# Experts of a two-layer trunk: rows 4 to 7 of down loaded directly behind rows 0 to 3

## The reference

```python
def _expert_choice_ffn(h, router, w_gate, w_up, w_down):
    b, t, _ = h.shape
    cap = CAPACITY_FACTOR * t // N_EXPERTS
    aff = jax.nn.softmax(jnp.einsum('btd,de->bte', h, router).astype(jnp.float32), axis=-1)
    top_w, top_i = lax.top_k(jnp.swapaxes(aff, 1, 2), cap)
    bidx = jnp.arange(b)[:, None, None]
    xe = h[bidx, top_i]
    a = jnp.einsum('becd,edf->becf', xe, w_gate)
    u = jnp.einsum('becd,edf->becf', xe, w_up)
    y = jnp.einsum('becf,efd->becd', jax.nn.silu(a) * u, w_down) * top_w[..., None].astype(h.dtype)
    return jnp.zeros_like(h).at[bidx, top_i].add(y)
```

## Time and profile before

| | us |
|---|---|
| median of 3 runs | 3843.08 |
| lowest, highest | 3839.8, 3844.74 |
| the profiled execution's run | 3849.27 |
| its span, first to last instruction | 3847.5 |

### The profile page before, as it was taken

One profiled execution on the slowest core, in us unless ns is written; L12 is line 12 of the kernel. 1 busy time (PEld: TensorE's weight loads), 2 busy tenths in 40 slices (PEclk: granted clock), 3 DMA queues, 4 the chain that ended last, 5 costly groups with the idle time before them and its releaser, 6 DMA issues.

```text
span 3847.5 us, 59293 instructions
## 1 busy us (share of the span) xinstructions
PE 3193.2 (83%) x24115; PEld 2288.9 (59%) x24115; DVE 2297.4 (60%) x2989; ACT 1735.3 (45%) x2289; POOL 397.6 (10%) x100
## 2 busy tenths in 40 slices
PE   6899977866949999999978999777668588888887
PEld 1365767755426666666633666677553466666665
DVE  0141465577247887888831233656772688888887
ACT  1111431222127777777720114312222477777776
POOL 0000000000011222221100000000000133332222
PEclk9999978856969999999999999778558789889889
DMA  7310000000158999999964110000013589999996
GB/s 247 108 60 33 1 1 3 3 2 2 44 210 321 352 355 354 358 352 354 357 247 142 45 55 1 1 3 3 2 45 121 217 337 346 341 349 349 351 344 255
DMA packets 180704, 680.24 MB, mean 177 GB/s; under 512 B 15435, under 2 KB 25759, under 8 KB 180383
## 3 DMA queue, kind: packets, MB, share of 16 engines
q1 hardware_dynamic: 166088, 637.81, 43.5%
q0 software_dynamic: 6144, 20.98, 2.4%
q10 hardware_dynamic: 8283, 18.67, 1.2%
HBM read 656.44 MB, written 20.97 MB: 176 GB/s over the span
## 4 chain that ended last, share of the span: by engine, by line
PE 57%; DVE 16%; ACT 9%; issue 9%; DMA 7%; ACTq 1%; SPq 0%; DVEq 0%; POOL 0%; PEldq 0%
PE ps L718 13%; PE ps L1865 10%; PE ps L1835 7%; PE ps L1290 5%; ACT hi L1947 4%; PE ps L1635 4%; DMA gu<-in_moe_w_up 3%; PE ps L657 3%; PE ps L973 2%; DMA arena<-in_w_mod 2%; ACT arena L1956 2%; DVE gu_lo L2098 2%; DMA gu<-in_moe_w_gate 2%; PE ps L1873 1%; PE ps L951 1%
## 5 line engine op out<-in xcount | busy, mean ns | idle before, releaser
L2098 DVE TENSOR_TENSOR gu_lo<-gu,hi 128x2816 fp32r<-128x2816 f32 x256 | 783.5, 3091 | 273.4 <-ACT hi L1947 249.6
L1947 ACT ACTIVATE hi<-gu 128x2816 fp32r<-128x2816 f32 x256 | 643.7, 2550 | 141.6 <-DMA gu<-in_moe_w_up 115.3
L1835 PE MATMUL ps<-hi,xsplit 128*96 128x512 f32 (+3 forms) x2304 | 562.9, 390 | 45.4 <-DVE arena L2112 20.5
L718 PE MATMUL ps<-arena 128*128 128x512 f32 (+2 forms) x1536 | 503.4, 488 | 7.1 <-PE ps L718 4.3
L1835 PEld LDWEIGHTS ps<-hi,xsplit 128*96 128x96 f32 (+1 forms) x2304 | 396.0, 177 | 159.9 <-ACT hi L1947 28.4
L2098 DVE TENSOR_TENSOR down_lo<-down,hi 128x1024 fp32r<-128x1024 f32 (+1 forms) x256 | 403.9, 1620 | 45.7 <-ACT hi L1947 45.7
L1835 PE MATMUL ps<-gu_lo,xsplit 128*96 128x512 f32 (+3 forms) x1536 | 381.3, 384 | 54.5 <-DVE gu_lo L2098 54.3
L718 PEld LDWEIGHTS ps<-arena 128*128 128x128 f32 x1536 | 289.7, 190 | 212.3 <-issue 187.0
L1947 ACT ACTIVATE hi<-down 128x1024 fp32r<-128x1024 f32 (+1 forms) x256 | 344.0, 1377 | 158.2 <-PE ps L1865 158.2
L1835 PEld LDWEIGHTS ps<-gu_lo,xsplit 128*96 128x96 f32 (+1 forms) x1536 | 262.1, 177 | 150.7 <-DVE gu_lo L2098 92.6
L2180 POOL DMA_INDIRECT arena<-xn_rows,row_of x32 | 88.0, 2751 | 2158.0 <-DVE row_of L2089 2153.3
(11 more groups left out here) (290 smaller groups left out, 4443.9 us busy)
## 6 DMA issues: line engine op xcount, KB each, us to landing
gu<-in_moe_w_gate SPq DMA_DIRECT2D x256, 704.0 KB, 14.9
gu<-in_moe_w_up SPq DMA_DIRECT2D x256, 704.0 KB, 5.0
down<-in_moe_w_down SPq DMA_DIRECT2D x64, 2048.0 KB, 13.5
arena<-in_w_mod SPq DMA_DIRECT2D x24, 2048.0 KB, 8.0
down<-in_moe_w_down SPq DMA_DIRECT2D x32, 1536.0 KB, 17.0
arena<-in_w_in SPq DMA_DIRECT2D x6, 2048.0 KB, 8.0
arena<-in_w_out SPq DMA_DIRECT2D x4, 2048.0 KB, 10.2
arena<-in_w_in SPq DMA_DIRECT2D x4, 1536.0 KB, 6.6
```

The source lines that it names most:

```text
L718: ins = nc.tensor.matmul(out, lhsT=lhs, rhs=rhs, start=(f == 0), stop=(f == KT - 1))
L1835: ins = nc.tensor.matmul(ps[0:lhs.shape[1], 3 * m + b, 0:n], lhsT=lhs, rhs=w[:, c0 + 512 * b:c0 + 512 * b + n], start=(row == 0 and stage ...
L1947: nc.scalar.activation(hi_part(p, is_last), whole(p), ACT.Copy).then_inc(hi_a.sem, 1)
L2098: nc.vector.tensor_tensor(lo_part(p), whole(p), hi_part(p, is_last).bitcast(F32), ALU.subtract) \
```

## The change

In the loop and behind it, SP's call `downs(e, 1)` moves up: from behind `gate_up(e + 1, 1)` in the loop, and from behind `gate_up(NE - 1, 7)` at the end, to directly behind `downs(e, 0)`.

```diff
             with sp.Fori(1, NE - 1) as e:
                 downs(e, 0)
+                downs(e, 1)
                 gate_up(e, 6)
                 gate_up(e, 7)
                 gate_up(e + 1, 0)
                 gate_up(e + 1, 1)
-                downs(e, 1)
                 downs(e, 2)
                 for k in range(2, 6):
                     gate_up(e + 1, k)
             downs(NE - 1, 0)
+            downs(NE - 1, 1)
             gate_up(NE - 1, 6)
             gate_up(NE - 1, 7)
-            downs(NE - 1, 1)
             downs(NE - 1, 2)
```

## The result

The changed kernel takes 3854.76 us (median of 8 runs, 3839.36 to 3862.54); the kernel before, run beside it, 3843.68 (median of 8). The ratio is 1.0028, with a 95% interval of 1.0015 to 1.0041. So it is 11 us slower, and clearly so. 3843 was forecast, no change, with a range up to 3855: the time lies at the range's very end, 0.24 us inside it, and it moved where no move was forecast.

The account below looks back on a forecast made before the run. Prediction: the expert stages lean on both PE and DMA, neither full, with ACT alone waiting for weights. All terms summed to 0 on the 3847.5 us span; from the three-run median of 3843.08 it gave 3843 us, range 3834 to 3855.

Parts of the forecast that it names:

- What bounds the kernel, and where the queue stands still: Both expert stages: PE and DMA both lean, neither full; the DMA engines stand nearly still once per expert.
- Removed from the old place: 0.: Behind k1': d1 leaving moves later transfers up 5.1 us, but nobody waits for them; gain 0.
- The wait at the new place: 0.: SP's queue behind d0: d1's wait ends 8.0 and 7.4 us before k6's release, delaying nobody; 0.
- The transfer, first layer: 0.: Ahead of k6: d0 comes 5.1 us earlier, d1 takes 5.1, the 2.7 us hole stays; change 0.
- The transfer, second layer: -6 to +9, taken as 0.: Ahead of k6: room 5.3 us against 5.1 needed; -6 to +9 us over 15 experts, taken as 0.
- the bound for a lagging transfer: Second layer's k6: some 0.6 us later if one of sixteen DMA engines lags as in the first layer.
- k6 queues behind d1: Second layer: d0 no earlier, k6 1.4 us late for each of 15 experts; 21 us, 3864 us; chance 0.07.
- about as much as it is late: PE behind ACT's wait for k6: a delay of k6 costs PE about as much as it is late.
- the likeliest case: Whole kernel: nothing moves that anyone waits for; 3843 us, bounds 3837 to 3852; chance 0.82.
- a lower rate of d1: Second layer: d1 served at 350 GB/s takes 6.0 us, 0.7 over the room; 10 us, 3853 us; chance 0.03.
- The gate pairs land earlier.: First layer: k0' and k1' land earlier without d1; at most 20.6 us of gate waits go, 3822 us; chance 0.07.

Follow-up runs that it names:

- the half: Against the kernel before: d1 cut in two in both layers, only the second layer's first half moved ahead of k6; 3844.67 us, ratio 1.0006.
- the kernel with both fillers: Against the kernel before: 6 unused matmuls ahead of the gate's transposes and 12 ahead of the first down group, second layer; 3799.44 us, 0.9878.
- e2: Against the kernel before: d1 moved in the second layer's stage alone; 3851.68 us, ratio 1.0024.
- e9: Against the kernel before: d1 cut in two in both layers, three quarters moved ahead of k6 in the second layer only; 3842.34 us, 0.9996.
- e10: As e2, against the kernel before, but the second layer's d1 reads the expert before's rows, 5.5 MiB lower; 3845.49 us, ratio 0.9999.
- e11: e2 repeated for a second trace: d1 moved in the second layer alone, reading its own rows; 3836.41 us, one run.
- e12: e2 repeated, against the kernel before: d1 moved in the second layer alone, reading its own rows; 3847.62 us, ratio 1.0014.
- e1: Against the kernel before: d1 moved in the first layer's stage alone; 3845.71 us, ratio 1.0005.
- e13: As e10, against the kernel before: d1 moved in the second layer alone, reading 5.5 MiB lower; 3843.24 us, ratio 0.9994.

## Why the prediction was wrong

*What bounds the kernel, and where the queue stands still.* Right. ACT waits for k6 and the gate pairs and never for down, also after. (An expert of the first layer takes 50.8 us by the earlier trace rows, 1511.87 - 1461.10, not 51.0; nothing hangs on it.)

*Removed from the old place: 0.* Right, as far as the half and the first layer alone test it: what moved up shows neither gain nor cost.

*The wait at the new place: 0.* Right. d1 went out 5.6 us behind d0 in the first layer and 3.6 in the second (5 to 6 had been said), 7 to 8 us ahead of k6, and k6 kept its distance of 13.6 and 11.0 us to d0.

*The transfer, first layer: 0.* Right: 1.0005, and of the hole of 2.7 us 2.0 stayed.

*The transfer, second layer: -6 to +9, taken as 0.* This is the step that failed. The usual expert was right: 5.3 us of room against 5.1, d1 landing 12.7 us behind d0's issue by the working, 12.8 in the trace for expert 6 (issued 3.6 us behind d0, landed in 9.2), k6 of expert 5 in 5.3 us. But a sum that comes out at 0.2 us has no room for a spread, and the bound for a lagging transfer was taken as 0.6 us from one landing of the first layer. k6 was 1.4 to 2.4 us later than usual in four experts of fifteen, and over all fifteen 0.7 us later than before, a little over that bound. A transfer's parts on the sixteen DMA engines report one by one: in expert 7 of the change 31 of the 32 parts of k6's two loads were there 6.5 us after the first issue and the last at 8.2; in the kernel before the last came 0.1 us behind the one ahead of it, at 5.8. Before, a hole of 3.7 us stood ahead of k6 in which an engine that was behind could catch up. The lag starts ahead of k6 but grows mostly in it: in experts 3, 7 and 11 the last part of d1 is there 13.1 to 13.3 us behind d0's issue, where nine of the other ten experts from 2 to 14 have 12.5 to 12.9, and the last part of k6 is 1.4 to 2.4 us late. A late d1 isn't enough by itself: in expert 1 it is there at 13.9, and k6 is 0.6 us late. The rival "k6 queues behind d1" had this place and this sign, but its price was a mean delay of 1.4 us in all experts; the measured one is a larger delay in a few.

*The price of a late k6: "about as much as it is late".* Wrong too: 1.7 us late costs 3.4 us, since PE stands still for longer and then mostly runs at 0.50 for longer; with PE kept busy at that wait it costs 2.1. The window of the second stage had shown a granted clock of 0.90 in the earlier trace rows, and it was quoted and not asked what made it so. With a price of twice the delay the upper bound of 9 us would have been 18, and the likeliest case would no longer have been "no change" alone.

*The range.* That 3854.76 lies within 3834 to 3855 is luck: the likeliest case ended at 3852, and the range was carried on to 3855 for a lower rate of d1, which is not what happened.

*The rate.* 413 GB/s for d1's stretch was about right (392 over the 5 us ahead of expert 7's k6, 418 over the 8 us ahead of expert 6's), and the mean of an expert rose to 377 GB/s over 47 us in the kernel with both fillers. The limit of about 358 GB/s that the Trainium skill gives ("DMA: Bandwidth & Descriptors", section Specifications) is exceeded there over a whole expert; the measurement decides. At 392 d1 takes 5.4 us, 0.1 more than the room, so the rival's 0.7 us in every expert, by a rate of 350, was not what happened.

*"The gate pairs land earlier."* ACT's gate waits of the first layer fell from 20.6 to 12.0 us, and the first stage was 1.7 us shorter, but the timed runs of the first layer alone show no gain, and in the traces of e2, e9, e10, e11 and e12, whose first layer is in the order of before, that stage takes 706.4 to 712.7 us.

## What to carry to other kernels

A hole in a queue ahead of the one transfer that an engine waits for is a reserve against late landings; before it is filled, compare its length with the spread of the landings, not with their mean. Where the granted clock of a stretch is under 1.00, a longer wait of PE can cost more than its length (here 3.4 us for 1.7), so a delay is priced from an experiment that sets it, with the clock low and with PE kept busy. And such a stretch is a place for a gain: eighteen small matmuls per expert of the second layer without any use made this kernel 1.2% faster, and six of them gave most of it.

## What the runs showed of the hardware

- PE's clock: around waits of 1.49 us and of 2.73 us (expert 7 of before) the granted clock was 0.50 (1.2 GHz) for 3 and about 6 us; around one of 3.92 us (expert 7 of the change), for at least 9. It isn't so each time: with waits of 1.76 and 2.7 us expert 8 of e1 had 0.97. With the waits filled it was 1.00 for the whole of expert 7, and its time fell from 51.3 to 47.2 us.
- The landing of the same two loads behind the same queue took 5.1 or 8.4 us (expert 11 of e13 and e12), and shifting another load's source by 5.5 MiB was enough to go from one to the other. In the 4 us from 2 us behind the issue, five of the late ones ran at 330 to 386 GB/s, seven in time at 397 to 418.
- The transfers of one core ran at a mean of 377 GB/s over an expert of 47 us.
